# Moving half of two modulations from ScalarE to VectorE in a two-layer diffusion backbone with experts

## The reference, cut to what matters

```python
px = _modulate(x, sh1, sc1) @ w_in[l]          # h * (1 + scale) + shift, per column
... # Fourier mixer | differential attention | spatial gating, concatenated
x = _layernorm(DEEPNORM_ALPHA * x + g1 * (mix_x @ w_out[l]), ln_g[l, 0], ln_b[l, 0])
hx = _modulate(x, sh2, sc2)
yx = _moe(hx, _route(hx, w_router, router_bias), moe_w1[l], moe_w3[l], moe_w2[l])
x = _layernorm(DEEPNORM_ALPHA * x + g2 * yx, ln_g[l, 1], ln_b[l, 1])
```

## Time and profile before

| | |
|---|---|
| median of 3 runs | 1134.85 us (1132.71 to 1135.66) |
| the profiled execution | 1137.95 us, span 1136.4 us |
| mean granted clock of TensorE | 0.939 of full |
| busy, share of the span | PE 86%, DVE 31%, POOL 22%, ACT 20% |
| chain that ended last | PE 65%, DMA 21%, DVE 5%, issue 5%, ACT 2% |
| modulation pieces (L854) | 112, mean 471 ns, 40.7 us busy |
| HBM traffic | 330.43 MB moved, mean 291 GB/s |

### The profile page before, as it was taken

One profiled execution on the slowest core, in us unless ns is written; L12 is line 12 of the kernel. 1 busy time (PEld: TensorE's weight loads), 2 busy tenths in 40 slices (PEclk: granted clock), 3 DMA queues, 4 the chain that ended last, 5 costly groups with the idle time before them and its releaser, 6 DMA issues.

```text
span 1136.4 us, 24584 instructions
## 1 busy us (share of the span) xinstructions
PE 980.2 (86%) x9166; PEld 551.1 (48%) x9167; DVE 349.0 (31%) x853; ACT 222.8 (20%) x564; POOL 247.5 (22%) x460
## 2 busy tenths in 40 slices
PE   4999999999978998998988869998997878786584
PEld 2444656564455555554554434645645434443343
DVE  1003032742364521221221186024334512111115
ACT  1311010860251111111110122203613000100010
POOL 0200000010015443444333410000101323332232
PEclk9999999889999999999999979999997879988897
DMA  8997383654156686789999995537575999999993
GB/s 325 369 410 296 127 317 121 250 235 172 60 205 228 260 306 246 283 319 394 389 390 403 395 353 217 169 138 271 236 300 209 340 398 401 394 397 404 400 389 115
DMA packets 88584, 330.43 MB, mean 291 GB/s; under 512 B 10433, under 2 KB 12913, under 8 KB 63953
## 3 DMA queue, kind: packets, MB, share of 16 engines
q1 hardware_dynamic: 66736, 282.14, 65.0%
q0 software_dynamic: 20320, 46.43, 11.4%
q10 hardware_dynamic: 1472, 1.12, 0.3%
HBM read 302.66 MB, written 27.00 MB: 290 GB/s over the span
## 4 chain that ended last, share of the span: by engine, by line
PE 65%; DMA 21%; DVE 5%; issue 5%; ACT 2%; SPq 2%; POOL 1%; DVEq 0%; ACTq 0%
PE PS L1763 17%; DMA W<-in_moe_w 15%; PE PS L2027 15%; PE PS L1929 7%; PE PS L2042 6%; PE PS L1676 3%; DMA XT<-in_moe_w 3%; PE PS L1779 3%; PE PS L1705 3%; PE PS L2016 2%; PE PS L1879 2%; PE PS L1891 1%; PE PS L2034 1%; DMA W<-in_w_ada 1%; SPq L589 1%
## 5 line engine op out<-in xcount | busy, mean ns | idle before, releaser
L2027 PE MATMUL PS<-W,EX 128*32 128x256 f32 x2720 | 178.6, 417 | 56.6 <-DMA W<-in_moe_w 29.1
L1763 PE MATMUL PS<-W,XT 128*128 128x512 f32 (+1 forms) x480 | 189.3, 554 | 0.4 <-ACT XT L854 0.4
L2027 PEld LDWEIGHTS PS<-W,EX 128*32 128x32 f32 x2720 | 94.4, 120 | 125.7 <-issue 80.5
L1763 PEld LDWEIGHTS PS<-W,XT 128*128 128x128 f32 x480 | 91.3, 192 | 94.2 <-issue 91.8
L719 POOL TENSOR_TENSOR RSTD<-VAR,HALF 128x1 f32<-128x1 f32 (+1 forms) x24 | 18.3, 765 | 451.2 <-DVE VAR L1144 451.2
L829 ACT ACTIVATE AT<-EX 64x512 f32<-64x512 f32 x64 | 40.4, 631 | 386.0 <-PE PS L2016 326.1
L1511 DVE COPY EX<-PS 128x256 f32<-128x256 f32 x66 | 28.0, 424 | 277.1 <-PE PS L2027 277.1
L2027 PE MATMUL PS<-RAB,EX 128*32 128x256 f32 x736 | 89.3, 398 | 25.8 <-DMA XT<-in_moe_w 14.7
L750 POOL DMA_DIRECT2D y_rows<-AT x128 | 63.5, 497 | 119.5 <-DVE AT L1524 58.7
L2027 PE MATMUL PS<-XT,EX 128*32 128x256 f32 x736 | 89.3, 398 | 0.0
L750 POOL DMA_DIRECT2D y_rows<-EX x120 | 59.5, 497 | 116.7 <-DVE EX L1524 53.6
(11 more groups left out here) (265 smaller groups left out, 1047.5 us busy)
## 6 DMA issues: line engine op xcount, KB each, us to landing
W<-in_moe_w SPq DMA_DIRECT2D x65, 2048.0 KB, 21.7
W<-in_w_ada SPq DMA_DIRECT2D x24, 2048.0 KB, 12.1
RAB<-in_moe_w SPq DMA_DIRECT2D x10, 2048.0 KB, 21.8
XT<-in_moe_w SPq DMA_DIRECT2D x10, 2048.0 KB, 26.5
H<-in_moe_w SPq DMA_DIRECT2D x10, 2048.0 KB, 24.8
W<-in_w_in SPq DMA_DIRECT2D x7, 2048.0 KB, 18.6
W<-in_w_out SPq DMA_DIRECT2D x4, 2048.0 KB, 19.9
EX<-xg_rows POOLq DMA_DIRECT2D x128, 64.0 KB, 5.6
```

What stands on the lines that cost most here:

```text
L1763: mm = pe.matmul(ps[:, 0:cw], XT[:, k, P * t:P * t + P], w[:, k, :], start=(k == 0), stop=(k == KD - 1))
L2027: mm = pe.matmul(UP_PS[o:o + ROWS, 0:256], rows, w[:, 256 * a:256 * a + 256], start=(k == 0), stop=(k == KD - 1), tile_position=(0, o))
```

## The change

VectorE gets its own `modulated`: it waits for the same columns of scale and shift and for the same PSUM bank, and writes the same blocks of XT with a tensor_scalar (multiply by MA, add MB). `on_vector` names the halves that ScalarE leaves out: the second half of the last tile in front of the router (tile 3 in layer 0, tile 1 in layer 1), and the second half of tile 0 of layer 1 at the change of layers. VectorE does the router's ones behind the last tile's normalisation, and the one at the change of layers inside `mix(1)`, between its first and second operation. That is three halves, twelve pieces out of 112.

```diff
+            def on_vector(key):
+
+                return key[1:] in [(1, 0, 1)] if key[0] == "hT" else key[2:] == (tiles(key[1]) - 1, 1)
+
...
                         for hf in range(2):
-                            modulated(job + (hf,), 0, t)
+                            if not on_vector(job + (hf,)):
+                                modulated(job + (hf,), 0, t)
...
                     for hf in range(2):
-                        modulated(("xT", L, t, hf), 1, t)
+                        if not on_vector(("xT", L, t, hf)):
+                            modulated(("xT", L, t, hf), 1, t)
...
+            def modulated(key, kind, t):
+
+                dve.wait_ge(S["hx_cols" if kind else "h1_cols"], val("hx_cols" if kind else "h1_cols", key[1], 0))
+                ps = full(dve, key)
+                hf = key[3]
+                for k in range(4):
+                    n = 4 * hf + k
+                    ins = dve.tensor_scalar(XT[:, n, P * t:P * t + P], ps[:, P * k:P * k + P],
+                                            MA[:, kind, n, t // 2:t // 2 + 1], MB[:, kind, n, t // 2:t // 2 + 1], ALU.mult, ALU.add)
+                ins.then_inc(freed(key), 1)
...
                     normalise(L, "ln1", t, S["ln1_norm"])
 
+                modulated(("xT", L, T - 1, 1), 1, T - 1)
                 for t in range(T):
                     read(dve, ("rt", L, t))
...
                                                         in1=kept_rows(t), op0=ALU.mult, op1=ALU.add), t)
+                        if t == 1:
+                            modulated(("hT", L + 1, 0, 1), 0, 0)
                         link(dve.scalar_tensor_tensor(out=g0, in0=g1, scalar=WE[:, 1, t:t + 1], in1=g0,
```

## The result

The changed kernel took 1129.1 us (median of 20 runs, 1123.11 to 1133.81), the kernel before 1133.26 us (20 runs beside it, 1126.78 to 1142.1). The ratio is 0.9949, with a 95% interval of 0.9934 to 0.9965: 5.8 us of 1133, between 4.0 and 7.5. The plain difference of the medians is 4.2 us. Over all the runs of this study (56 of the changed kernel, 194 of the one before) the means differ by 4.85 us, give or take 0.9 (95%); one run of the kernel before that took 3260 us, in the slow state, is left out.

A forecast was written before the change was run, and what follows sets the result against it. The chain through ScalarE's modulations ahead of the routers was taken as binding, though expert stages end on the weight stream. Terms 1.30 + 0.15 + 0.87 + 0.15 + 0.30 = 2.8 us off 1134.85 gave 1132.0; range 1129.2 to 1136.0.

The forecast's parts named there:

- moves the expert stage and its stream as a block: Both layers: time gained before the router shifts expert stage and weight stream together, so a microsecond there should reach the end.
- the sum: Terms for both routers, their following products and the change of layers: 1.30 + 0.15 + 0.87 + 0.15 + 0.30 = 2.8 us.
- No queue is passed: Change of layers: POOL's reciprocal roots come 2.1 us later with nothing behind them, SP sees nothing; the delay costs nothing.
- VectorE's four pieces: Four tensor_scalars of 128x128 out of PSUM on VectorE take 1.0 us, between 0.98 and 1.39.
- Rival D: VectorE's four cost 1.39 us and start 0.3 later each time; each router gives 0.7 less: 1133.4; chance 0.06.
- Layer 0's router: Last tile before layer 0's router: sums start 1.30 us earlier, between 0.9 and 1.4, plus 0.15 for the product behind.
- the bonus: Short product behind the router's copy comes before the clock falls: 0 to 0.32 us in layer 0, taken as 0.15.
- Layer 1's router: Last tile before layer 1's router: sums start 0.87 us earlier, between 0.5 and 1.0, plus 0.15 for the product.
- Change of layers: First tile of layer 1: TensorE's 0.39 us idle before the first projection goes; gain 0.2 to 0.39, taken as 0.3.
- B: Expert weights or load queue set the layer's end; routers' gain is waited away, leaving 1134.5; chance 0.14.
- C: Layer 0: longer TensorE idling before the mask sums lowers the clock over spreading and gathering, costing 3.3 us: 1135.4; chance 0.10.
- A: Layer 1: the earlier, denser router keeps or regains the high clock over gathering, 1.8 us more: 1130.2; chance 0.20.

The follow-up runs named there:

- one wait on SyncE: Kernel before, with SyncE holding layer 1's first load behind the scattered rows until ScalarE has activated the first expert: ratio 0.998, by means 2.0 us faster.
- empty writes on VectorE: Kernel before, with 15 one-column memsets on VectorE, five at each place where the change has its pieces: ratio 0.9996, by means 1.7 us faster.
- the two delays of 5.72 us: Kernel before, with sixteen more scratch modulations on ScalarE ahead of layer 0's router, or of layer 1's: ratios 1.0053 and 1.0035.
- the version with the routers' part and SyncE's wait: Kernel before, with both routers' halves on VectorE, nothing at the change of layers, and SyncE's wait before layer 1's first load behind the scattered rows: ratio 0.9986.

## Why the prediction was wrong

**The step that failed** is the one that says what the router gains "moves the expert stage and its stream as a block", and with it the sum, which has terms for the three edited places only. In layer 1 the stage did not move as a block: it became shorter. Behind its first expert the changed kernel lacks a standstill of TensorE (4.92 us to 2.01) and the gap in the stream that follows. By traces this is worth 3.7 us (261.68 less 258.00); by times, 2.0 give or take 1.5 (one wait on SyncE) and 1.7 give or take 1.6 (empty writes on VectorE, 1.0 give or take 1.9 against the runs beside them). The whole change less its local terms is 4.85 - 2.14 = 2.7 us, or 2.3 with the 0.43 behind the first projection, and the times allow that. The row was there to see: the trace of before had a 4.92 us "issue" in the expert stage of layer 1, and the forecast had no term for it. "No queue is passed", it said; the queue that mattered was one of kind "instruction". That the change would shorten the standstill, nothing in that trace could have told.

Part of the miss is the base and no mechanism. The forecast took its 2.8 us off 1134.85, the median of three runs; the 20 runs of the same kernel beside the result have 1133.26. Of the 2.9 us between the forecast 1132.0 and the measured 1129.1, that is 1.6.

The local terms, in order:

- **VectorE's four pieces.** Forecast 1.0 us, bounds 0.98 and 1.39; measured 1.36 and 1.37. Each lasts 0.402 us, longer than the longer of the two nearest rows (0.347). I had taken the row with the same operand place and size, 0.292; the pointer operands, two here, were the better guide. Four in 1.36 is one start in (1.36 - 0.402) / 3 = 0.32 us, so they overlap by 0.08. The sentence that the prediction took from the Trainium skill (VectorE: DVE Perf Modes, "The DRAIN you can't avoid"), that the next operation waits for an empty pipe, would have it 4 x 0.402 = 1.61 us, 0.25 more than the trace. But the prediction left out what the same section adds, that a next operation that is not held starts earlier; the start every 0.32 us fits that, and so do the six in 1.77 us of the rows before, if these are such operations, which no run here shows. Rival D's price for the four was thus nearly right, and its chance of 0.06 too small for that part; its total of 1133.4 is not what came.
- **Layer 0's router.** Forecast 1.45, found 0.70 over the traces. The four pieces take 0.36 of it. More lies in the clock, which the average mixes. In three traces without the change and two with it, the granted clock stayed at 1.00 through the turns and the sums, as in the earlier trace rows; there the interval fell from 12.40 or 12.41 to 11.15 and 11.17, by 1.25: 1.03 from turn to sums (3.70 to 2.67), and 0.21 by the product behind the sums, 0.40 us for 0.61, which is the bonus that the forecast priced at 0.15. In four traces without and five with it, the clock was at its low level over the sums (granted 0.50); there it fell from between 12.95 and 13.07 to between 12.34 and 12.44, by 0.64, with the product at 0.61 in all. The profiled execution of the changed kernel is one of these five, and the forecast's rows were of the other kind.
- **Layer 1's router.** Forecast 1.02, found 0.98. Between traces with the same clock as in the earlier trace rows (turns of 1.95 to 1.97 us, sums of 0.64) it fell from 11.80 and 11.83 to 11.00 to 11.02, by 0.81: 0.61 from turn to sums, where the forecast had 0.87 and the dearer pieces take 0.36 off, and 0.16 by the product (0.40 for 0.56), where it had 0.15. So the mechanism is the one forecast, and the closeness of 0.98 to 1.02 is in part luck: in the other three traces with the change the turns took 1.13 to 1.28 us.
- **Change of layers.** Forecast 0.30, found 0.46, and 0.43 behind it, where the traces scatter by 0.9, so that this is no more than a hint. The lateness on VectorE was covered, as reckoned: counted from the turn of tile 0, the last tile was normalised 1.9 us later, and 1.0 us of the cover was left in the profiled execution, where the forecast had 2.0.

**The rivals.** B (the stream hides it) is refuted for a loss by the two delays of 5.72 us, which cost 5.3 and 5.4; for a gain it is only unlikely. C (the clock takes it back in layer 0) did not happen: from mask sums to first expert there every trace has 10.85 us. A (the clock adds in layer 1) is not seen as a rule: from mask sums to first expert that layer took 8.62 to 9.10 us with the routers' part and 8.63 to 9.50 without, on average 0.3 us less. None of them is the standstill. The chances of the forecast and the four rivals add up to 1.00, so nothing was left for a gain outside their terms; the range was too narrow below.

**Open.** Why the traces give 3.7 us to the standstill and the times only about 2; profiled executions may be no fair sample. Why the version with the routers' part and SyncE's wait is 2.6 us slower than the changed kernel. Why the scattered rows come later when q14's packet falls beside them: counted from the mask sums of layer 1, the first rows are gathered at 13.2 to 13.6 us in the eight traces with the early packet and at 12.4 to 12.8 in the ten without it, so the two go together in every trace, but that one makes the other is argued, not shown. (The short standstill of the change of layers alone is no exception: its rows came at 12.6 us from the mask sums; its first expert was early, 8.63 us behind them.) That q14 carries VectorE's program rests on the empty writes alone, that q8 carries TensorE's on the order of events in 18 traces. And the three measured parts (routers 0.8, change 0.85, empty writes 1.7) sum to 3.35, give or take 2.9, against 4.85 give or take 0.9: compatible, not a proof.

## What to carry to other kernels

Where an engine stands still on "issue" in the middle of a long run of equal instructions, look at the queues of kind "instruction" beside it: here a fetch that came late behind weight loads went with 3.3 us more of standstill, and 15 more instructions on another engine were enough to move it. A change of well under a per cent should be compared with padded versions of the kernel before, by traces as well as by times, with instructions that reach the engine, ahead of crediting its mechanism. And two halves put on two engines end when the slower one ends, so price the newcomer by its dearest operand kind.

## What the runs showed of the hardware

A tensor_scalar of 128x128 floats out of PSUM with two per-partition pointers takes 0.402 us on VectorE, and four in a row 1.36 to 1.37 us; the same work as activations on ScalarE takes 0.470 us each (mean of 100), and four in a row 1.51 us. With fifteen one-column writes on VectorE, ten of them 200 us and more ahead, a packet on q14 came 2 us behind layer 1's first expert and not 24 to 25, and the stream there moved 394 GB/s and not 283. TensorE's standstill in the second expert ended 1.2 to 1.5 us behind the end of a packet on q8 in all 18 traces. One program's local intervals differ from execution to execution with the granted clock (layer 0's turn to mask sums 11.15 us at a clock of 1.00 and 12.44 at 0.50 over the sums, in the changed kernel), which is as much as the edits themselves are worth.
